# Long convolutions: weights earlier, an own buffer for the second half's output, folds earlier, matrix splits on GpSimd

## The reference, cut to what matters

```python
def hyena_filters(T, w1, b1, w2, b2, w3, b3, w4, freq):
    # z: time and 32 sines and cosines of it, three small sine layers give hdn (T x 64)
    filt = (hdn @ w4).reshape(T, 2, D_INNER)                 # forward, backward
    filt = filt * jnp.exp(-t * deltas[None, :])[:, None, :]  # decay by channel
    filt = filt / (jnp.sum(jnp.abs(filt), axis=(0, 1), keepdims=True) + 1e-6)
    return filt[:, 0], filt[:, 1]

def bidir_long_conv(v, h_fwd, h_bwd, skip):
    n = 2 * T
    taps = jnp.concatenate([h_fwd, jnp.zeros((1, C)), h_bwd[:0:-1]], axis=0)
    y = irfft(rfft(v, n=n, axis=1) * rfft(taps, n=n, axis=0)[None], n=n, axis=1)[:, :T]
    return y + v * skip

v = bidir_long_conv(v * x1, h_fwd, h_bwd, skip)
y = v * x0
return (y * silu(z)) @ w_out
```

## Time and profile before

| | us |
|---|---|
| median of 3 runs (lowest to highest) | 2777.58 (2775.21 to 2777.95) |
| the profiled execution: time, span of the trace | 2777.97, 2776.2 |
| PE busy | 2401.9 (87%) |
| DVE busy | 1695.4 (61%) |
| ACT busy | 1291.3 (47%) |
| POOL busy | 801.0 (29%) |

### The profile page before, as it was taken

How to read it: one execution, slowest core, us unless ns; L and a number is a source line. 1 busy time by engine, 2 the same in 40 slices (tenths; PEclk the granted TensorE clock), 3 DMA queues, 4 the chain that set the end, 5 groups by cost and what they waited for, 6 DMA issues and landing times.

```text
span 2776.2 us, 38209 instructions
## 1 busy us (share of the span) xinstructions
PE 2401.9 (87%) x15755; PEld 2124.7 (77%) x15755; DVE 1695.4 (61%) x2584; ACT 1291.3 (47%) x2074; POOL 801.0 (29%) x501
## 2 busy tenths in 40 slices
PE   4999997888899899999998968678888783999994
PEld 3999996887899888999897736567766673877873
DVE  3444545878753766666666535884465514888885
ACT  3444433434432556555555223333244202888884
POOL 1211112444431222222221114103100012776772
PEclk8999997989899999999999979898799985999997
DMA  4232321000042222222222304114110432788873
GB/s 142 77 92 87 120 72 47 16 31 31 12 125 84 62 73 74 77 67 68 76 68 51 94 15 110 48 47 114 51 46 23 140 118 70 262 284 286 300 261 146
DMA packets 228328, 275.52 MB, mean 99 GB/s; under 512 B 42792, under 2 KB 194953, under 8 KB 215610
## 3 DMA queue, kind: packets, MB, share of 16 engines
q1 hardware_dynamic: 213642, 264.64, 30.3%
q0 software_dynamic: 14512, 8.45, 1.0%
HBM read 283.24 MB, written 31.05 MB: 113 GB/s over the span
## 4 chain that ended last, share of the span: by engine, by line
PE 52%; DVE 23%; ACT 11%; issue 6%; POOL 5%; DMA 2%; SPq 1%; POOLq 0%; DVEq 0%; ACTq 0%
PE ps L92 15%; PE ps L93 14%; PE ps L94 14%; ACT whi L98 2%; DVE wlo L102 2%; ACT sp L106 1%; PE ps L1758 1%; POOL wlo L102 1%; DVE prods L1108 1%; DVE work L2479 1%; POOL xg L3548 1%; DVE m L2477 1%; PE ps L458 1%; DVE p L2053 1%; POOL yd L3554 1%
## 5 line engine op out<-in xcount | busy, mean ns | idle before, releaser
L92 PE MATMUL ps<-hn_h,whi 128*128 128x264 f32 (+3 forms) x2296 | 711.5, 310 | 53.4 <-POOL wlo L102 30.1
L93 PE MATMUL ps<-hn_l,whi 128*128 128x264 f32 (+3 forms) x2296 | 692.9, 302 | 0.0
L94 PE MATMUL ps<-hn_h,wlo 128*128 128x264 f32 (+3 forms) x2296 | 692.2, 301 | 0.0
L92 PEld LDWEIGHTS ps<-hn_h,whi 128*128 128x128 f32 (+1 forms) x2296 | 440.3, 192 | 88.1 <-issue 33.5
L94 PEld LDWEIGHTS ps<-hn_h,wlo 128*128 128x128 f32 (+1 forms) x2296 | 440.0, 192 | 15.3
L93 PEld LDWEIGHTS ps<-hn_l,whi 128*128 128x128 f32 (+1 forms) x2296 | 440.4, 192 | 11.6 <-issue 0.2
L102 POOL TENSOR_TENSOR wlo<-wraw,whi 128x2048 fp32r<-128x2048 f32 (+1 forms) x46 | 167.8, 3648 | 684.7 <-ACT whi L98 684.7
L102 DVE TENSOR_TENSOR wlo<-wraw,whi 128x2048 fp32r<-128x2048 f32 (+1 forms) x122 | 253.7, 2080 | 92.6 <-ACT whi L98 92.4
L98 ACT ACTIVATE whi<-wraw 128x2048 fp32r<-128x2048 f32 (+1 forms) x168 | 265.0, 1578 | 52.6 <-PE ps L94 51.0
L709 DVE SCALAR_TENSOR_TENSOR c<-ub,vec,c 128x528 f32<-128x528 f32 x48 | 45.3, 944 | 140.7 <-ACT c L106 140.7
L106 ACT ACTIVATE ub<-ps,vec 128x528 f32<-128x528 f32 x48 | 33.7, 702 | 165.8 <-PE ps L94 165.8
(11 more groups left out here) (719 smaller groups left out, 6542.3 us busy)
## 6 DMA issues: line engine op xcount, KB each, us to landing
wraw<-in_w_gate_up SPq DMA_DIRECT2D x33, 1024.0 KB, 7.1
wraw<-in_hy_w_in SPq DMA_DIRECT2D x32, 1024.0 KB, 5.6
wraw<-in_da_w_in SPq DMA_DIRECT2D x64, 512.0 KB, 4.2
ex_raw<-in_w_gate_up SPq DMA_DIRECT2D x31, 1024.0 KB, 6.3
ex_raw<-in_w_down SPq DMA_DIRECT2D x17, 1024.0 KB, 5.8
wraw<-in_w_down SPq DMA_DIRECT2D x15, 1024.0 KB, 6.9
wraw<-in_w_in SPq DMA_DIRECT2D x14, 1024.0 KB, 5.5
wraw<-in_hy_w_out SPq DMA_DIRECT2D x8, 1024.0 KB, 7.9
```

Of the source, the lines that this page charges most:

```text
L92: e.matmul(out, lhsT=l[0], rhs=r[0], start=start, stop=False)
L93: e.matmul(out, lhsT=l[0], rhs=r[1], start=False, stop=False)
L94: return e.matmul(out, lhsT=l[1], rhs=r[0], start=False, stop=stop)
```

## The change

1. `prods` and `Y_h` get other addresses. `y_of(c, h)` gives `prods` for h = 1 in every chunk. The second half's output then waits for DVE's own `im` of z = 4, the first half's for the `yl` of the first half one chunk before, and the products of z = 0 of the next chunk wait for `yl` of the second half.
2. `vector_w4(c + 2)` stands ahead of `vector_turned`. ACT does `w4h` after the first half's `d`, both halves' `d` before both `yh`, and POOL does `w4l` ahead of the gate products.
3. `vector_filter` is split: `vector_differ` (time zero, sums) stands ahead of the products, `vector_larger` (L952 before) behind them. Time zero is one DVE instruction after an ACT one that halves the row.
4. The norm is summed into the bank of the turned signal (`vb[0]`); the first filter step no longer waits for the norm; `vector_filter_end` stands at the turn's end.
5. POOL folds h = 1 at z = 1, ahead of that step's `Y_l`.
6. ACT's absolute value of filter step 4 stands behind the product of z = 3, and the second step of each pair waits for the first's absolute value.
7. Ahead of the first turn, POOL takes the low parts of matrices 2 to 5, both folds come first, and chunk 0's norm comes behind PE's first filter transform.

```diff
     def y_of(c, h):
-        return prods[:].rearrange("p a b c -> p (a b c)")[:, 0:T] if (c, h) == (7, 1) else sq[1][:]
+        return prods[:].rearrange("p a b c -> p (a b c)")[:, 0:T] if h else sq[1][:]
+    def lo_by_matrix(m):
+        return ("cv.vec", "mats", m) if m < 2 else ("cv.pool", "mats", m)
...
     def vector_filter(e, w, c, step):
         hp_free(w, c, i)
+        if m:
+            w.wait_ge("cv.act", "abs0", c, i)
         e.tensor_tensor(hp[0:n, m, :], fbank[0:n, :], ab, ALU.mult).then_inc(*mark("cv.vec", "hp", c, step))
-        if m == 0:
-            return
+    def vector_differ(e, w, c, i):
+        w.wait_ge("cv.vec", "hp", c, 2 * i + 1)
         if i == 0:
-            e.tensor_tensor(x, x, y, ALU.add).then_inc(*mark("cv.vec", "zero0", c))
-            ts(e, x, x, 0.5, None, ALU.mult).then_inc(*mark("cv.vec", "zero1", c))
-            e.tensor_copy(y, x).then_inc(*mark("cv.vec", "zero", c))
+            w.wait_ge("cv.act", "half", c)
+            e.scalar_tensor_tensor(x, x, 0.5, y, ALU.mult, ALU.add).then_inc(*mark("cv.vec", "zero", c))
...
+    def vector_larger(e, w, c, i):
+        w.wait_ge("cv.act", "abs", c, i)
         e.tensor_tensor(ab, ab, abs0[0:n], ALU.max).then_inc(*mark("cv.vec", "ab", c, i))
...
     def vector_freq(e, w, c, z):
-        if c_ >= 0:
+        if c and z == 0:
+            w.wait_ge("cv.pool", "yl", c - 1, 1)
+        elif c_ >= 0:
             w.wait_ge("cv.vec", "im", c_, z_)
...
     def vector_back(e, w, c, h):
-        if (c, h) == (7, 1):
-            w.wait_ge("cv.vec", "im", 7, 4)
-        elif h or c:
-            w.wait_ge("cv.pool", "yl", *((c, 0) if h else (c - 1, 1)))
+        if h:
+            w.wait_ge("cv.vec", "im", c, 4)
+        elif c:
+            w.wait_ge("cv.pool", "yl", c - 1, 0)
...
     def scalar_conv(e, w):
                 scalar_product(e, w, c, z)
+                if c < 7 and z == 3:
+                    scalar_filter(e, w, c + 1, 4)
             scalar_back(e, w, c, 0)
             if c < 6:
                 scalar_w4(e, w, c + 2)
+            scalar_back(e, w, c, 1)
             scalar_out(e, w, c, 0)
-            scalar_back(e, w, c, 1)
             scalar_out(e, w, c, 1)
...
     def vector_conv(e, w):
+            if c < 6:
+                vector_w4(e, w, c + 2)
             if c < 7:
-                vector_turned(e, w, c + 1)
-                vector_sums(e, w, c + 1, 0)
-                vector_sums(e, w, c + 1, 1)
+                vector_turned(e, w, n)
+                vector_larger(e, w, n, 2)
+                vector_sums(e, w, n, 0)
+                vector_sums(e, w, n, 1)
             vector_back(e, w, c, 0)
             vector_skip(e, w, c, 0)
             if c < 7:
-                vector_sums(e, w, c + 1, 2)
-                vector_filter_end(e, w, c + 1)
-            if c < 6:
-                vector_w4(e, w, c + 2)
+                vector_sums(e, w, n, 2)
             vector_back(e, w, c, 1)
             vector_skip(e, w, c, 1)
+            if c < 7:
+                vector_filter_end(e, w, n)
...
     def gpsimd_conv(e, w):
         gpsimd_fold(e, w, 0, 0)
+        gpsimd_fold(e, w, 0, 1)
...
+        matrix(2)
+        matrix(3)
         gpsimd_w4(e, w, 1)
+        matrix(4)
+        matrix(5)
...
             for z in range(5):
-                if c < 7:
-                    if z in (0, 2):
-                        gpsimd_fold(e, w, c + 1, z // 2)
+                if c < 7 and z < 2:
+                    gpsimd_fold(e, w, c + 1, z)
                 gpsimd_freq(e, w, c, z)
-            gpsimd_back(e, w, c, 0)
             if c < 6:
                 gpsimd_w4(e, w, c + 2)
+            gpsimd_back(e, w, c, 0)
             gpsimd_back(e, w, c, 1)
```

More of the change, by code:

```diff
@@ L788, in build @@
     vTl = [sb(f"vT_l{i}", [128, 2, 256], F32R, RING + x) for i, x in enumerate((53248, 55296))]
-    vTx = sb("vT_x", [128, 2, 256], F32R, HT + 14336)
-    Y_h = sb("Y_h", [128, 5, 2, 256], F32R, HT)
-    prods = sb("prods", [128, 2, 2, 256], F32, HT + 10240)
+    vTx = sb("vT_x", [128, 2, 256], F32R, HT + 4096)
+    prods = sb("prods", [128, 2, 2, 256], F32, HT)
+    Y_h = sb("Y_h", [128, 5, 2, 256], F32R, HT + 6144)
     tl_x = sb("tl_x", [128, 4, 256], F32R, PH2 + 4544)
@@ L904, in tensor_filter @@
         elif c:
-            w.wait_ge("cv.vec", "norm", c - 1)
+            w.wait_ge("cv.vec", "hp", c - 1, 5)
         for s in range(2):
@@ L922, in hp_free @@
             w.wait_ge("cv.vec", "sum", c_, i_)
+            w.wait_ge("cv.act", "abs0", c_, i_)
     def vector_filter(e, w, c, step):
@@ L959, in scalar_filter @@
             act(e, dec[0:n, i].rearrange("p s c -> p (s c)"), hp[0:n, 1, :], ACT.Abs).then_inc(*mark("cv.act", "abs", c, i))
+            if i == 0:
+                y = hp[0:1, 1, 0:256]
+                w.wait_ge("cv.act", "abs", c, i)
+                act(e, y, y, ACT.Copy, scale=0.5).then_inc(*mark("cv.act", "half", c))
             return
@@ L978, in tensor_filter_end @@
                 for s in range(2):
-                    t = e.matmul(fbank[:, h:h + 1], lhsT=dec[:, i, s, 128 * h:128 * h + 128], rhs=once if i == 2 else ones[:, 0:1],
+                    t = e.matmul(vb[0][:, h:h + 1], lhsT=dec[:, i, s, 128 * h:128 * h + 128], rhs=once if i == 2 else ones[:, 0:1],
                                  start=(i == 0 and s == 0), stop=(i == 2 and s == 1))
@@ L985, in vector_filter_end @@
         w.wait_ge("cv.pe", "norm", c)
-        ts(e, r, fbank[:, 0:2], 1e-6, None, ALU.add).then_inc(*mark("cv.vec", "norm", c))
+        ts(e, r, vb[0][:, 0:2], 1e-6, None, ALU.add).then_inc(*mark("cv.vec", "norm", c))
         w.wait_ge("cv.vec", "norm", c)
@@ L1006, in tensor_turned @@
                 w.wait_ge("cv.vec", "vT", c - 1, i)
+            w.wait_ge("cv.vec", "norm", c - 1)
         w.wait_ge("cv.pool", "pads")
@@ L1211, in tensor_conv @@
                 tensor_freq(e, w, c, z, 1)
+                if c == 0 and z == 0:
+                    tensor_filter_end(e, w, 0)
                 if c < 7 and z in (1, 3):
@@ L1235, in scalar_conv @@
             scalar_filter(e, w, 0, step)
+            if step in (1, 3):
+                matrix(step + 1)
+                matrix(step + 2)
             if step == 2:
@@ L1239, in scalar_conv @@
         scalar_w4(e, w, 1)
-        for m in range(2, 6):
-            matrix(m)
         w.wait_ge("left")
@@ L1251, in scalar_conv @@
                 scalar_freq(e, w, c, z)
-                if c < 7 and z == 3:
-                    scalar_filter(e, w, c + 1, 4)
-                elif c < 7 and z == 4:
+                if c < 7 and z == 4:
                     scalar_turned(e, w, c + 1)
@@ L1273, in matrix @@
             w.wait_ge("cv.act", "mats", m)
-            lo_part(e, mats_l[:, m], mraw[:, m], mats_h[:, m]).then_inc(*mark("cv.vec", "mats", m))
+            lo_part(e, mats_l[:, m], raw_matrix(m), mats_h[:, m]).then_inc(*mark("cv.vec", "mats", m))
         vector_w4(e, w, 0)
-        for step in range(6):
-            if step < 2:
-                matrix(step)
-            elif step == 2:
-                w.wait_ge("cv.act", "tl")
-                lo_part(e, tl_x[32:41], tl_raw[32:41], tl_x[32:41]).then_inc(*mark("cv.vec", "tl"))
-            vector_filter(e, w, 0, step)
-            if step == 2:
-                vector_turned(e, w, 0)
+        matrix(0)
+        vector_filter(e, w, 0, 0)
+        matrix(1)
+        vector_filter(e, w, 0, 1)
+        w.wait_ge("cv.act", "tl")
+        lo_part(e, tl_x[32:41], tl_raw[32:41], tl_x[32:41]).then_inc(*mark("cv.vec", "tl"))
+        vector_differ(e, w, 0, 0)
+        vector_filter(e, w, 0, 2)
+        vector_larger(e, w, 0, 0)
+        vector_turned(e, w, 0)
+        vector_filter(e, w, 0, 3)
+        vector_differ(e, w, 0, 1)
+        vector_filter(e, w, 0, 4)
+        vector_larger(e, w, 0, 1)
+        vector_filter(e, w, 0, 5)
+        vector_differ(e, w, 0, 2)
+        vector_w4(e, w, 1)
         for i in range(3):
             vector_sums(e, w, 0, i)
-        vector_w4(e, w, 1)
-        vector_filter_end(e, w, 0)
-        for m in range(2, 6):
-            matrix(m)
+        vector_larger(e, w, 0, 2)
         w.wait_ge("cv.act", "lf")
```

72 lines of the change are left out of this document (42 added, 30 removed).

## The result

The changed kernel takes 2754.41 us (median of 4, 2751.9 to 2759.33) against 2777.51 before: ratio 0.9921, 95% interval 0.9903 to 0.9938. Timed again in more rounds it gave 0.9917 (0.9896 to 0.9938). The forecast was 2761.5, in a range of 2750 to 2772.

The account below looks back on a forecast made before the run. No engine fills the 42.6 us turn; order and waits bound it, the chain lying on DVE and POOL. Terms -15.3 - 0.8 - 1.0 + 0.7 + 0.35 = -16.0 us gave 2761.5 us, range 2750 to 2772.

Parts of the forecast that it names:

- The boundary: From b, the start of vT_l, to the next products: 15.55 us against 17.7, 2.1 saved, ending on POOL and ACT.
- The skip product and the rule: At the boundary, by the skill's rule, the skip product is held by POOL's w4l: 0.4 us, bounds 0 and 1.3.
- the forecast 1.0 us of the last chunk: Last chunk: both d ahead of both yh, so the 1.08 us idle at 803.57 falls to about nothing.
- PE's gap and low clock: Before the first taps: PE's 4.4 us stop vanishes, and the 1.2 GHz stretch behind it goes too.
- PE then works almost without a break: Argument against PE falling to 1.2 GHz inside the turn in the new order.
- The slower rival: PE falls to 1.2 GHz through last transform and back products: +4.1 us a turn, about 2788 us; chance 0.06.
- Inside the turn: From products of z = 0 to next b, 24.9 us before: holds, moved larger and freed sums add to -0.45.
- the smaller terms: Inside the turn: larger moved (0.6 each), step 5's hp waiting for ACT +0.7, time zero's small instructions (0.31 each) gone.
- The fold: Fold h = 1 at z = 1 takes turns with both sums, +0.9 (bounds 0 and 1.8); none at z = 2, -0.55.
- The second rival: The folds hold nobody, so +0.75 and +0.9 go, seven times 1.65: 2750 us; chance 0.12.
- Before the first turn: First hp of chunk 1 waits for dec, loaded after chunk 0's later norm: 0.7 us lost, bounds -0.3 and +2.7.
- The sum: All terms, -15.3 - 0.8 - 1.0 + 0.7 + 0.35, give -16.0 us, with everything behind the convolution moving along.

Follow-up runs that it names:

- before, both: Kernel before the change with only the early weights and the own place for the second half's output: turn 40.33 us, one execution of 2766.76 us.
- three edits: Changed kernel with second gate product on DVE, chunk 0's norm early, second fold at z = 2: 2737.85 us, ratio 0.987 to the kernel before.

## Why the prediction was right, step by step

The direction and the places were right; the gain in the turns was a third too small. The turn in its stretches, in us, from the products of one step to those of the next; b is the end of the last imaginary part, where the boundary starts:

| stretch | before | before, both | changed | forecast change | measured change |
|---|---|---|---|---|---|
| z = 0 to 1 | 6.81 | 7.10 | 6.30 | +0.5 | -0.5 |
| z = 1 to 2 | 3.89 | 3.89 | 4.48 | +0.6 | +0.6 |
| z = 2 to 3 | 6.73 | 6.73 | 5.76 | -1.15 | -1.0 |
| z = 3 to 4 | 5.53 | 5.53 | 5.33 | -0.4 | -0.2 |
| z = 4 to b | 1.91 | 1.92 | 1.92 | 0 | 0 |
| b to z = 0 | 17.68 | 15.18 | 14.97 | -2.1 | -2.7 |

- **The boundary**: forecast -2.1 us, measured 17.68 to 14.97, -2.7. The new bound is the one named, the chain of two gate products and two `yl`, and its length is the forecast 6.7: 594.2 to 600.9. It starts 0.6 sooner. `w4l` did ask before the second `fl_l` was done and came behind it, as forecast. It held the skip product by 0.1 us and not 0.4 (0.86 for 0.77); the other 0.3 lie in the instructions ahead of the first output, 5.34 us for 5.6.
- **The skip product and the rule.** By the Trainium skill, page "SBUF — State Buffer", section "Who interferes with whom", a DVE instruction with two SBUF inputs contends with a GpSimd instruction that reads SBUF. The trace agrees in the last chunk, where a `yl` starts at 779.01 and runs for 1.34 us. DVE's timeline of the changed kernel there:

```profile
776.74 0.77 DVE L1199 SCALAR_TENSOR_TENSOR sq<-vv,vec,sq 128x528 f32<-128x528 f32 x1
...
779.09 1.82 DVE L1199 SCALAR_TENSOR_TENSOR prods<-vv,vec,prods 128x528 f32<-128x528 f32 x1
```

The same skip product takes 0.77 free and 1.82 beside it. That also eats the forecast 1.0 us of the last chunk: the gate product behind it starts at 780.95, 25.5 us after the chunk's first products, before 25.6 (805.30 less 779.68).
- **PE's gap and low clock.** The gap before the first taps is gone. The low clock is not, and here the prediction was wrong. The granted clock is 1.00 in two of seven turns, 0.96 in one and 0.91 in four. One of the four, and a stretch of it behind the back products, with PE's first taps of z = 0 at 633.66:

```profile
601.04:639.82 38.78, 35.27 (x266) 34.44 (x267) 31.00 (x48) 16.98 (x28) 20.51 (x23) 0.91 0.09 28
...
633.00:635.00 2.00, 2.00 (x12) 2.00 (x11) 1.93 (x6) 0.64 (x1) 1.25 (x1) 0.50 0.91 342
```

PE had worked without a break from 619 to 631 before that, so the argument "PE then works almost without a break" did not keep the clock up. Why it fell is open. It cost nothing: this turn is 38.78 us long, the one at clock 1.00 38.76, since POOL's chain ends later than PE's work. The slower rival needed the low clock under the back products; there it never was (the 48 ran from 621.49 to 627.6 in this turn, at clock 1.00). PE's gaps are under 1 us but for two of 1.9, where PE waits for a fold behind the products of z = 0.
- **Inside the turn**: forecast -0.45, measured 24.9 to 23.8, -1.1. The mis-sized terms are two holds by a fold. The real part of z = 0 is held by 0.3 (0.71) and not 0.75, and the two sums of z = 1 by 0.44 (1.73 for 1.29) and not 0.9. Each was priced at twice what the traces show or more, and together they make 0.9 us; the smaller terms missed the other way, by 0.3 in all. Time zero in one instruction came out near its forecast: the way from the first instruction to the sums falls from 1.6 to 0.5 us and ACT's half adds 0.45, so 0.6 is won where the terms had 0.5. Of the smaller terms `larger` is +0.6 at z = 1 to 2 as said, the wait of step 5 for ACT 0.77 for 0.7, and z = 2 to 4 together gained 1.2 for 1.55.
- **The fold** was counted as a loss of 0.9 at z = 1 against 0.55 won at z = 2. The loss is 0.44, and the 0.55 would have come without the move, from `larger` standing behind the products. The second rival's 1.65 was too much: the holds that it takes away are 0.3 and 0.44.
- **Before the first turn**: forecast 0.7 lost, bounds -0.3 and +2.7; measured 1.2 (39.3 for 38.1 us behind the first `w4s`), by the mechanism named. The first `hp` came 5.4 us after the load's issue at 477.47, where the forecast had 4.4. The weights' DMAs go right behind that load; whether they slow it was not tried. The 0.35 for the norm in the first turn does not show: that turn is 38.66 us long.
- **The sum**: first products of chunk 0 to those of chunk 7, 270.7 for 294.9 us: 24.3 less, forecast 15.8. The stage began 1.1 us sooner in this execution, before any changed instruction. So the convolution ends 24.4 us earlier. The execution's span is only 19.0 less. ACT's group of the expert stage's inputs starts at 2294.2 before and at 2271.5 after, 22.7 less; the last loads at 2744.5 and 2725.3, 19.2 less. No instruction there changed. In the second profiled execution of the same changed kernel the same stretch takes 451.5 us, in the first 453.8 (before 450.3), and the one with three edits 454.0. That the expert stage varies by such amounts is shown; what of it varies was not looked into. By the medians the change is 23.1 us against the forecast 16.

The 1.56 us between "both" and the changed kernel can be followed through the traces. At the boundary the second gate product no longer stands idle 0.78 us for the second output, as both `d` stand ahead of both `yh`, and `larger` adds 0.6. At z = 0 to 1 time zero gives 0.6 and `larger` 0.6, and the fold takes 0.44. At z = 1 to 2 `larger` takes 0.6. The real part of z = 2 gives 0.57. The rest of z = 2 to 4 gives 0.6: `larger` of z = 4 is now at the boundary, and what the freed sums of z = 4 win (1.06) goes to the later `hp` and the sums of z = 3. What stays open: ACT's order was not tried alone, so its 0.8 us is read from the traces and not shown by a run.

## What to carry to other kernels

Where two engines hold each other up, count the instructions that stand in line, not their microseconds: putting back two of 0.28 us cost 1.25 us with a fold beside them, about 0.6 by the traces without one. Two waits that cover each other must be taken away together, and trying each alone shows which hides the other (0 and 1.2 alone, 2.2 together). The same holds for undoing: where two edits take away one hold, undoing either alone shows nothing. When work is shifted to gain time ahead of a load, look first at what issues the load: here the norm that releases it was put later, and what was won ended in a wait of 5.5 us for a DMA.

## What the runs showed of the hardware

Read from the starts and lengths of the rows, DVE and POOL take turns. A POOL instruction that asks while DVE runs one of several queued instructions comes next, and DVE's following one waits until it is done: beside a fold two sums take 1.73 us, free 1.29. The halving at 571.30 above, with one operand, was held as well (0.72 for 0.28). POOL's own two-column copies are held too, 0.65 us for 0.18:

```profile
567.45 0.65 POOL L1010 COPY fold<-vv 128x2 f32<-128x2 f32 x1
...
569.36 0.18 POOL L1010 COPY fold<-vv 128x2 f32<-128x2 f32 x1
```

DVE instructions reading one operand from PSUM (`prods` at 128 rows 1.20 to 1.23 in every run, `hp` 0.67 to 0.69) were never held.

PE's granted clock fell to 0.50 (1.2 GHz) for 3 to 7 us at a time in the changed kernel, also right behind 12 us, 619 to 631, in which PE was busy throughout at clock 1.00. Turns with and without such stretches are equally long here (38.78 and 38.76), as another engine's chain ends last.
